# Sixteen-row steps of gathered expert rows: the twelve row buffers split 6 and 6 in place of 4 for U and 8 for V

## The reference

```
s1, i1 = top_k(s[:, :, 0], 16);  s2, i2 = top_k(s[:, :, 1], 16)
top, sel = top_k(s1 + s2 of all 256 pairs, 16)
idx  = take_along_axis(cidx, sel)             # 8 heads x 16 experts of 16384, for each token
g    = softmax(top)
u    = expert_u[idx]                          # rows of 1024 float32
act  = gelu(einsum('td,thkd->thk', c, u))
coef = g * act
out  = einsum('thk,thkd->td', coef, expert_v[idx])
```

## Time and profile before

| | |
|---|---|
| median of three executions | 4656.01 us |
| profiled execution | 4640.09 us |
| its span | 4638.6 us |
| third stage's gathers, first to last | 822 to 4416 us |
| TensorE busy, over the span | 76% |
| VectorE busy | 60% |
| POOL busy | 59% |
| ScalarE busy | 25% |
| traffic, mean | 292 GB/s, 1352.76 MB |

### The profile page before, as it was taken

The page is one execution under the profiler, slowest core; times in us unless marked ns, Lnnn a source line. Parts: engine busy times, 40 slices in busy tenths (PEclk is TensorE's granted clock), DMA queues, the critical chain, the costliest instruction groups (busy, mean ns, idle before and its releaser), DMA issues. The chain is left out here.

```text
span 4638.6 us, 34517 instructions
## 1 busy us (share of the span) xinstructions
PE 3545.3 (76%) x9836; PEld 1681.3 (36%) x9836; DVE 2793.5 (60%) x5456; ACT 1175.8 (25%) x2311; POOL 2728.2 (59%) x2372
## 2 busy tenths in 40 slices
PE   8997774578668678778778868887787788666678
PEld 3443332233334244234334424433442444222233
DVE  1111224667766866876777687777768676855423
ACT  0011330231331242143135114413421451111111
POOL 0000000677777777777778777877677666777700
PEclk9998777689889989989999999899899899988899
DMA  4112213899999999999999999999989998999931
GB/s 167 55 63 86 77 40 126 309 360 350 359 351 342 364 378 349 353 385 371 328 359 362 332 358 359 345 334 353 340 323 345 334 330 318 354 372 373 369 143 50
DMA packets 448240, 1352.76 MB, mean 292 GB/s; under 512 B 47312, under 2 KB 117840, under 8 KB 447056
## 3 DMA queue, kind: packets, MB, share of 16 engines
q0 software_dynamic: 333328, 1213.35, 70.5%
q1 hardware_dynamic: 114752, 137.54, 8.6%
HBM read 1321.87 MB, written 28.84 MB: 291 GB/s over the span
## 5 line engine op out<-in xcount | busy, mean ns | idle before, releaser
L828 PE MATMUL sum_ps<-v_rows,diag 128*128 128x512 f32 x3628 | 1912.8, 665 | 688.0 <-DMA v_rows<-expert_v_in,idx_tile 400.6
L1158 DVE CUSTOM_DVE_ANT_0 u_rows<-u_rows,c_rows 128x1024 f32<-128x1024 f32 x1152 | 1407.0, 1226 | 709.0 <-DMA u_rows<-expert_u_in,idx_tile 646.7
L715 POOL DMA_INDIRECT u_rows<-expert_u_in,idx_tile x1152 | 1319.2, 1145 | 567.9 <-issue 335.2
L726 POOL DMA_INDIRECT v_rows<-expert_v_in,idx_tile x1152 | 1355.0, 1176 | 376.0 <-issue 320.8
L828 PEld LDWEIGHTS sum_ps<-v_rows,diag 128*128 128x128 f32 x3628 | 703.6, 209 | 1644.8 <-issue 966.6
L1010 ACT ACTIVATE diag<-ident,coef 128x128 f32<-128x128 f32 x907 | 329.9, 394 | 849.1 <-PE sum_ps L828 522.6
L142 PE MATMUL proj_ps<-weights,aT 128*128 128x512 f32 x864 | 378.8, 597 | 9.9 <-ACT aT L171 9.9
L1172 DVE SCALAR_TENSOR_TENSOR acc<-v_rows,coef,acc 128x1024 f32<-128x1024 f32 x236 | 303.6, 1286 | 0.0
L771 PE MATMUL z_ps<-w_query_sb,arena 128*128 128x512 f32 x576 | 254.8, 596 | 1.1 <-ACT arena L972 1.1
L142 PEld LDWEIGHTS proj_ps<-weights,aT 128*128 128x128 f32 x864 | 163.1, 191 | 207.5 <-issue 195.2
L1021 ACT ACTIVATE arena<-z_ps,neg_max 128x128 f32<-128x128 f32 (+7 forms) x128 | 94.8, 740 | 491.6 <-DVE neg_max L1319 343.3
(11 more groups left out here) (167 smaller groups left out, 3188.8 us busy)
## 6 DMA issues: line engine op xcount, KB each, us to landing
u_rows<-expert_u_in,idx_tile POOLq DMA_INDIRECT x1152
v_rows<-expert_v_in,idx_tile POOLq DMA_INDIRECT x1152
weights<-w_in_in SPq DMA_DIRECT2D x6, 2048.0 KB, 19.6
qk_turned<-turned SPq DMA_DIRECT2D x36, 256.0 KB, 3.1
w_query_sb<-w_query_in SPq DMA_DIRECT2D x1, 8192.0 KB, 35.8
x<-x_all_in POOLq DMA_DIRECT2D x9, 512.0 KB, 3.5
arena<-x_all_in SPq DMA_DIRECT2D x9, 512.0 KB
arena<-g_ffn_in SPq DMA_DIRECT2D x9, 512.0 KB
```

What stands on the lines that cost most here:

```text
L715: pool.indirect_dma_start(u_rows[r % U_RING][:, :], None, ins["expert_u"], bass.IndirectOffsetOnAxis(ap=idx_tile[:, e % 2, at:at + 1], axis=0)
L726: pool.indirect_dma_start(v_rows[g % V_RING][:, :], None, ins["expert_v"], bass.IndirectOffsetOnAxis(ap=idx_tile[:, e % 2, at:at + 1], axis=0)
L828: mm = nc.tensor.matmul(sum_ps[:, half * W:(half + 1) * W], diag[:, by_tensor[g] % DIAGS, :], v_rows[g % V_RING][:, half * W:(half + 1) * ...
L1158: nc.vector.tensor_tensor_reduce(row, row, c_rows[e % 2][:, :], 1.0, 0.0, ALU.mult, ALU.add, dots[:, s % 2, r % TOP:r % TOP + 1]).then_inc ...
```

## The change

The constants that size the two sets of buffers change, and with them, in the waits quoted above, the row whose consumption a gather waits for. U row r waits for row r - 6 in place of r - 4, V row g for row g - 6 in place of g - 8. The total stays twelve buffers of 4 KB per partition, and twelve landing semaphores. No instruction is added, removed or moved on any engine: the rows of each engine's program are the same in number and order.

```
-U_RING, V_RING, DIAGS = 4, 8, 4
+U_RING, V_RING, DIAGS = 6, 6, 4
```

## The result

The change took 4696.22 us in the median of five executions (4684.53 to 4704.9), the kernel before 4656.01. The ratio is 1.0076 with a 95% interval of 1.0044 to 1.0109, about 35 us slower (the medians are 40 us apart). The forecast was 4684, 0.6% slower.

What follows compares the result with a forecast made beforehand. DMA transfers were taken to bound the gather stage, at 351 GB/s and a share of 0.95. Query steps' 16 us plus attention steps' 12 us gave +28 on the 4656 median, so 4684 us, range 4622 to 4745.

Steps and rivals of the forecast that it cites:

- The U waits go, V waits take their place: POOL's queue: waits for dots fall from 146.8 to under 30 us, waits for TensorE rise from 28.1 to 120 to 280.
- The query step, 16 us: Tiles 0 to 7: V gathers wait for rows behind a queries product, 2.0 us lost a tile, 16 us.
- The attention steps, 12 us: Attention steps without a U wait: V gathers wait for late rows, 0 to 3.5 us a tile, 1.5 taken, 12 us.
- The V cut, 28 us in all: V ring from eight to six: query step 16 us plus attention steps 12 us, +28 us.
- The U half, 0 us: U ring from four to six: alone worth 79 us at most or nothing; no gain booked, as V waits replace U waits.
- The shape of time: POOL's waits: a 5 us wait costs 0 to about 2.7 us of transfer, about half at the worse end.
- rival 2: V waits add up, late rows making TensorE later: 74 us slower, 4730; last gather over 46 us past 4416; chance 0.28.
- The rule of the Trainium skill: Cited under rival 3, transfers bind whatever the buffers: HBM limit about 358 GB/s, no change, 4656 within 10; chance 0.10.

Runs made afterwards that it cites:

- the control with 4 and 8: U_RING 4, V_RING 8 as in the kernel before, but only the first half of w_out's columns loaded and used for both halves; 0.9998 against the kernel before.
- The run with rows first: U 6, V 6, with TensorE adding rows before the third and fourth products of queries in the query step; 1.0048 against the kernel before.
- The run of 4 and 6: U_RING 4, V_RING 6, only the V half of the change, two row buffers left unused; 1.0056 against the kernel before.
- 6 and 8: U_RING 6, V_RING 8, only the U half of the change, with half of w_out loaded; 1.0039 against the kernel before.
- 8 and 8: U_RING 8, V_RING 8, sixteen buffers, with half of w_out loaded; 1.0095 against the kernel before.
- 6 and 6: The change itself, U_RING 6 and V_RING 6 in place of 4 and 8; 4696.22 us, 1.0076 against the kernel before.
- the filler runs: Four products with a zero tile added ahead of each step's first row on TensorE; 1.0074 with U 6, V 6 and 1.0014 with 4 and 8, against the kernel before.
- the lead held to four: Eight U and eight V buffers, half of w_out, but U row r's gather waits for the dot of row r - 4; 0.9968 against the kernel before.

## Why the prediction was right, and where it was not

The sign, the size and the range held: +28 us were forecast, about +35 measured. Point by point:

- **The U waits go, V waits take their place.** Right, and in the forecast size: waits for dots under 30 us (28.1), waits for TensorE between 120 and 280 (217.8), VectorE's waits for U rows unmoved (644.7), DMA share 0.95.
- **The query step, 16 us.** The V gathers at positions 9 and 13 wait for TensorE as worked out, 4.07 and 4.08 us in tile 5. For position 13 I had 3.8; for position 9 I gave no length and booked nothing. The gathers behind these waits took 1.40 and 1.56 us, where I had put the shortest, 0.94. By the starts of the first U gathers of steps 5 and 6 in the two profiles, this step grew by 17 us over the eight tiles. Two single profiles can't show that, though: the control with 4 and 8, the same rings, differs from the profile before by -8 us in this step and by +29 in step 7. The run with rows first doesn't price it either. The mechanism is shown, the 16 us are not.
- **The attention steps, 12 us.** The waits came (89 us for TensorE in these steps), but in the two profiles the four attention steps together grew by only 2 us, step 7, which I had not named, by 17, and tile 8 by 9. The 1.5 us a tile was a choice between 0 and 3.5, and no run shows it.
- **The V cut, 28 us in all.** The run of 4 and 6 isolates it: +26 us (14 to 38). My sum of 16 + 12 was the sum for this half. The total is right; as neither term is shown by itself, its coming out so near is in part luck.
- **The U half, 0 us.** This step failed, though in the change it weighs little. I had priced two more U buffers between a gain of 79 us and nothing, and took nothing, since "a gather cannot be early past a V gather that waits for a diagonal". That V waits hold POOL is right, and with eight V buffers too; but alone the two buffers cost 0.4% (6 and 8 against its control), four of them 1.0%. In the change the two halves come to 1.0076, where 1.0056 is the V cut's, so U's share is about 0.2%, 9 us, with an interval wide enough to hold 0. That two buffers more cost beside a V ring of six is therefore not shown. The bounds excluded a loss without a reason in the trace; they should have held one.
- **The shape of time.** I tied each wait to half its length in lost transfer. POOL's named waits grew by 43 us and the time from first to last gather by 48 (3593 to 3642). That the two agree is in part bookkeeping: POOL was as busy as before (2701 and 2700 us in the windows), so whatever the stretch gained had to be idle time of POOL. It doesn't show that the waits caused the loss.
- **The mark for rival 2** was that the last gather comes over 46 us later than 4416; it came at 4463.5, 48 later. By the medians of both kernels, 40 us apart, it was not reached. The profile before was of an execution of 4640 us, 16 under its median, the one after 12 under its own, so marks taken from one profile against another are that uncertain. Rival 2's mechanism, late rows that make TensorE later, isn't seen: TensorE's waits for V rows fell, from 400.6 to 372.2 us (and from 354.1 in the control to 271.0 with 8 and 8); what grew is its wait for diagonals, 164.8 to 192.4.
- **The rule of the Trainium skill** (DMA: Bandwidth & Descriptors, Where 436 GB/s comes from) that the HBM side, about 358 GB/s, binds a load from HBM would have had no change at all. The interval from 1.0044 excludes that. The change lowered the pace of the stage from 351 to 347 GB/s at an equal share: transfers did not bind alone.

What stays open is how the run-ahead costs time. Every gather and every dot stands in the same order, and a longer ring only removes waits; by the program's waits alone nothing could come later. What is left are the durations: of transfers, of instructions and of the way from one engine to another. The clock is excluded as the main cause for 6 and 6 by the filler runs, and was not tested for 8 and 8. One stall was seen in the profile of 8 and 8 that none of these explains: ScalarE's copy at L984 began at 1480.92, though its own last instruction had ended at 1470.31 and TensorE's transposes that it needs at 1473.98 by the profile, in which ends of MATMULs are modelled; TensorE then waited for the copy. First ScalarE, then TensorE:

```profile
1480.92 0.59 ACT L984 COPY arena<-group_ps 128x512 f32<-128x512 f32 x1 [10.61 <-remote]
```
```profile
1473.38 0.60 PE L798 MATMUL group_ps<-ident,arena 128*128 128x128 f32 x4
1473.82 1.88 PE L828 MATMUL sum_ps<-v_rows,diag 128*128 128x512 f32 x4
1481.56 1.65 PE L807 MATMUL out_ps<-keysT,arena 128*128 128x128 f32 x6 [5.86 <-ACT arena L984]
```

That is 6.9 us. It was not ScalarE that started late: in the trace's record of semaphores, the one that the copy waits for rose at 1480.90, and the one that TensorE raises behind a row at 1480.96. What came late is TensorE's completion or its signal; the trace doesn't tell which, nor why. Delays of this kind, from the modelled end on TensorE to the start of the idle consumer, over three pairs that can be matched one to one (L798 to L984, L807 to L988, L850 to L1319), sum to 83 us with 8 and 8, 56 with 6 and 8, 60 in the control and 37 with the lead held to four, and to 37 both before and after the change. They may be a part of what 8 and 8 lost; they don't explain the change. Whether VectorE's lead, the attention loads or the turn of steps makes the lumps was not separated.

## What to carry to other kernels

When one in-order queue feeds two rings, a wait seen on one ring doesn't say that this ring is short: look at what the next gather of the other ring would wait for in the same microsecond. Let the range for more run-ahead reach below zero too, and try it apart from the buffers, by changing the wait and not the allocation. And a consumer that is late in a few known places (behind a product of 7 us, behind a diagonal) needs its ring sized for those places and not for the mean; moving another row behind the late place moves the wait with it.

## What the runs showed of the hardware

- A wait of the issuing engine (POOL) can be worth having: sixteen buffers with U held to a lead of four ran at 0.9968, the same sixteen without that hold at 1.0095.
- In a 5 us window in which POOL issued nothing until the last 0.1 us, the DMA engines still moved 409 GB/s. Over the whole stage the pace was 351 before and 347 after.
- Filling TensorE's idle time with 576 recorded products raised its granted clock from 0.897 to 0.917 and shortened its row products from 677 to 659 ns, without a measurable gain (1.0074 against 1.0076): a busy share and a clock are no time.
